# A new order for the operands of the pooled output product, in the lists of four engines

## The reference

```
def pool_mixer(x, w_in, w_grp, scale, w_out):
    h = x @ w_in
    u, z = h[..., :D_POOL], h[..., D_POOL:]
    ...                      # windowed means of u in four groups of 512 columns
    m = jnp.stack(outs, axis=2).astype(x.dtype)
    m = jnp.einsum('bsgc,gcd->bsgd', m, w_grp).reshape(B, S, D_POOL) * scale
    return (m * jax.nn.silu(z)) @ w_out
...
x = layer_norm(DN_ALPHA * x + y, ln_g[i], ln_b[i])
```

## Time and profile before

| | before |
|---|---|
| median of 3 runs | 1892.69 us (1892.03 to 1895.65) |
| the profiled execution | 1892.69 us, span from first to last instruction 1890.9 us |
| PE busy | 1832.0 us, 97% |
| DVE, POOL, ACT busy | 1368.0, 1079.6, 640.4 us |
| granted TensorE clock, mean | 0.995 |
| stage of the change (group product of group 0 to the last product of group 2) | 1621.8 to 1808.7 us of the span |

### The profile page before, as it was taken

The page is one execution under the profiler, slowest core; times in us unless marked ns, Lnnn a source line. Parts: engine busy times, 40 slices in busy tenths (PEclk is TensorE's granted clock), DMA queues, the critical chain, the costliest instruction groups (busy, mean ns, idle before and its releaser), DMA issues. The chain is left out here.

```text
span 1890.9 us, 23532 instructions
## 1 busy us (share of the span) xinstructions
PE 1832.0 (97%) x8904; PEld 1538.9 (81%) x8904; DVE 1368.0 (72%) x1530; ACT 640.4 (34%) x1128; POOL 1079.6 (57%) x780
## 2 busy tenths in 40 slices
PE   7999999999999999999999999999999999999996
PEld 6889889987887888888877888787788888788875
DVE  6777135566677776586589989567888876799886
ACT  4422157773331111111133433415433343323314
POOL 3443322253039988798876875532565465577655
PEclk9999999999999999999999999999999999999998
DMA  6111110013231143233377441113233231943122
GB/s 174 45 48 44 52 21 20 20 56 123 90 101 64 59 145 112 78 112 112 111 266 250 152 134 45 45 45 122 94 112 108 101 134 73 350 155 108 71 89 89
DMA packets 121698, 195.25 MB, mean 103 GB/s; under 512 B 30064, under 2 KB 85872, under 8 KB 118528
## 3 DMA queue, kind: packets, MB, share of 16 engines
q1 hardware_dynamic: 121424, 193.34, 30.1%
q10 hardware_dynamic: 176, 0.59, 0.1%
HBM read 145.08 MB, written 48.82 MB: 103 GB/s over the span
## 5 line engine op out<-in xcount | busy, mean ns | idle before, releaser
L1106 PE MATMUL ps<-f_hi,ring_hi 128*128 128x512 f32 x384 | 149.7, 390 | 1.3 <-POOL ring_lo L983 1.3
L1106 PE MATMUL ps<-f_lo,ring_hi 128*128 128x512 f32 x384 | 149.4, 389 | 0.0
L1106 PE MATMUL ps<-f_hi,ring_lo 128*128 128x512 f32 x384 | 149.4, 389 | 0.0
L893 POOL TENSOR_TENSOR w_lo<-stage,w_hi 128x1024 fp32r<-128x1024 f32 x48 | 124.7, 2598 | 4.0
L1106 PE MATMUL ps<-d_w_hi,d_hid_hi 128*128 128x512 f32 x312 | 121.8, 390 | 4.2 <-DVE y L2602 1.4
L1106 PE MATMUL ps<-d_w_hi,d_hid_lo 128*128 128x512 f32 x312 | 121.5, 389 | 0.0
L1106 PE MATMUL ps<-d_w_lo,d_hid_hi 128*128 128x512 f32 x312 | 121.4, 389 | 0.0
L983 POOL TENSOR_TENSOR ring_lo<-w_sum,ring_hi 128x512 fp32r<-128x512 f32 x80 | 117.2, 1465 | 6.7
L890 POOL TENSOR_TENSOR cols<-ones 128x1 f32<-128x1 f32 x48 | 26.1, 544 | 164.8 <-PE ps L1106 146.8
L1046 POOL TENSOR_TENSOR ring_lo<-w_sum,ring_hi 128x512 fp32r<-128x512 f32 x60 | 94.6, 1586 | 42.9 <-ACT ring_hi L2007 42.9
L1907 ACT ACTIVATE f_copy<-ps 128x512 f32<-128x512 f32 x60 | 35.3, 597 | 223.8 <-PE ps L1106 204.9
(11 more groups left out here) (442 smaller groups left out, 5707.1 us busy)
## 6 DMA issues: line engine op xcount, KB each, us to landing
d_raw<-hid_rows SPq DMA_DIRECT2D x37, 512.0 KB, 4.4
stage<-in_w_up SPq DMA_DIRECT2D x22, 512.0 KB, 4.5
wd_raw<-in_w_down SPq DMA_DIRECT2D x22, 512.0 KB, 4.9
raw_w<-in_w_gate SPq DMA_DIRECT2D x20, 512.0 KB, 4.9
stage<-in_w_in SPq DMA_DIRECT2D x18, 512.0 KB, 3.7
stage<-in_pool_w_in SPq DMA_DIRECT2D x16, 512.0 KB, 5.1
raw_w<-in_pool_w_in SPq DMA_DIRECT2D x16, 512.0 KB, 5.0
m_rows<-u_row SPq DMA_DIRECT2D x16, 512.0 KB, 2.6
```

The lines of the kernel that those rows point to most:

```text
L893: g.tensor_tensor(lo, stage[:, h, :], hi.bitcast(F32), ALU.subtract).then_inc(parted[h], 1)
L1106: last = mm(out_ap, l, r, start=(start and j == 0), stop=(stop and j == n - 1), skip_group_check=onto)
```

## The change

The same operations are done. What is changed is where some of them stand in four lists.

- **SP.** In the last round of the stage before (i = 7), the four loads of `wo_raw` for group 0 stood before the store of `z_buf`, in the block order 0, 2, 1, 3. They now stand behind it, in the order 0, 1, 3, 2.
- **DVE.** In group 0 the four `out_sums` stood after `gated` 4, after `gated` 6, after Q1's additions and after Q6's; in the groups 1 and 2 the first three stood after `gated` 1, 2, 3, and the fourth after Q6's additions. Now all groups have them after `gated` 1, 2, 3 and 4. The four `pool_rows_lo` of the next group stood after Q2 (one), Q7 (two) and Q3 (one); now they stand after Q5, Q7, Q3 and Q4, one each. The twelve `out_both_add` stood two after Q3, four after Q4 and six among the `gated` of group 3; now they stand two after Q7, three after Q3, three after Q4 and four in group 3.
- **ACT.** The high part of Q6's weights now comes before the rows of Q2, and the four `pool_rows_hi`, which stood in one piece after Q5's rows, are spread behind Q7 (two), Q3 and Q4.
- **POOL.** The low parts of Q2's and Q6's weights each move ahead of one operation on rows.

```
@@ sp_program, round i == 7
                     z_load(0, 0)
                     z_load(0, 1)
-                    sp.wait_ge(prod_full, quad_full(LAST_Q, 5))
-                    for b in (0, 2, 1, 3):
-                        wo_load(0, b)
                 sp.wait_ge(zs_ready, 4 * i + 4)
                 sp.dma_start(z_dram[i], z_buf[:].rearrange("p b n -> p (b n)")).then_inc(z_stored, 16)
...
+            sp.wait_ge(prod_full, quad_full(LAST_Q, 5))
+            for b in (0, 1, 3, 2):
+                wo_load(0, b)
@@ pool_program
                 out_weight_lo(i, Q1)
+                out_weight_lo(i, Q2)
                 out_rows_lo(i, Q1)
-                out_weight_lo(i, Q2)
+                out_weight_lo(i, Q6)
                 out_rows_lo(i, Q2)
-                out_weight_lo(i, Q6)
                 out_weight_lo(i, Q5)
@@ act_program
                 out_rows_hi(g, Q1)
+                out_weight_hi(g, Q6)
                 out_rows_hi(g, Q2)
-                out_weight_hi(g, Q6)
                 out_weight_hi(g, Q5)
                 out_rows_hi(g, Q6)
                 out_rows_hi(g, Q5)
-                pool_rows_hi(g + 1)
-                for o in (Q7, Q3, Q4):
-                    out_weight_hi(g, o)
-                    out_rows_hi(g, o)
+                out_weight_hi(g, Q7)
+                out_rows_hi(g, Q7)
+                pool_rows_hi(g + 1, (0, 1))
+                out_weight_hi(g, Q3)
+                out_rows_hi(g, Q3)
+                pool_rows_hi(g + 1, (2,))
+                out_weight_hi(g, Q4)
+                out_rows_hi(g, Q4)
+                pool_rows_hi(g + 1, (3,))
@@ dve_program
-            SUMS_AFTER = ((4, 6), (1, 2, 3))
-            BOTH = {Q3: (0, 1), Q4: (2, 3, 4, 5)}
...
                     gated(g, j)
-                    if j in SUMS_AFTER[g > 0]:
-                        out_sums(g, SUMS_AFTER[g > 0].index(j))
+                    if 1 <= j <= 3:
+                        out_sums(g, j - 1)
+                    if j == 4:
+                        out_sums(g, 3)
...
-                        if g == 0:
-                            out_sums(g, 2)
                     if o == Q2:
                         g_sums(g, 3)
-                        pool_rows_lo(g + 1, 0)
                     if o == Q6:
                         out_rows_low(g, Q7)
-                        out_sums(g, 3)
                     if o == Q5:
                         out_rows_low(g, Q3)
-                    if o == Q7:
-                        pool_rows_lo(g + 1, 1)
-                        pool_rows_lo(g + 1, 2)
-                    if o == Q3:
-                        pool_rows_lo(g + 1, 3)
-                    if g == STD_G - 1:
-                        for j in BOTH.get(o, ()):
+                    if o >= Q5:
+                        pool_rows_lo(g + 1, o - Q5)
+                    if g == STD_G - 1 and o >= Q7:
+                        for j in ((), (0, 1), (2, 3, 4), (5, 6, 7))[o - Q5]:
                             out_both_add(j)
```

More of the change, by code:

```diff
@@ L760, in z_load @@
                 sp.dma_start(z_in[:, e, :, :].rearrange("p b n -> p (b n)"), z_dram[2 * g + e]).then_inc(z_back, 16)
-            def wo_load(g, b):
-                r0, n = GW * PHASE[g] + 256 * (b // 2), b % 2
-                src = pw_out[r0:r0 + 256, n * HALF:(n + 1) * HALF].rearrange("(k p) n -> p k n", p=P)
-                sp.dma_start(wo_raw[b][:], src).then_inc(wd_in[b], 16)
             load(T_PG, cols_tile(w_pg, 0))
@@ L803, in sp_program, with wo_load @@
                     z_load(0, 1)
-                    sp.wait_ge(prod_full, quad_full(LAST_Q, 5))
-                    for b in (0, 2, 1, 3):
-                        wo_load(0, b)
                 sp.wait_ge(zs_ready, 4 * i + 4)
                 sp.dma_start(z_dram[i], z_buf[:].rearrange("p b n -> p (b n)")).then_inc(z_stored, 16)
+            def wo_load(g, b):
+                r0, n = GW * PHASE[g] + 256 * (b // 2), b % 2
+                src = pw_out[r0:r0 + 256, n * HALF:(n + 1) * HALF].rearrange("(k p) n -> p k n", p=P)
+                sp.dma_start(wo_raw[b][:], src).then_inc(wd_in[b], 16)
+            sp.wait_ge(prod_full, quad_full(LAST_Q, 5))
+            for b in (0, 1, 3, 2):
+                wo_load(0, b)
             sp.wait_ge(prod_full, quad_full(LAST_Q, 6))
@@ L2062, in first_block_rows, with pool_rows_hi @@
                 f(u_row[0][:, HALO:HALO + HALF], ps[:, 0, :], ACT.Copy).then_inc(c11_ready, 1)
-            def pool_rows_hi(g):
+            def pool_rows_hi(g, parts=range(4)):
                 if g:
                     act.wait_ge(grp_full, 8 * g)
-                for k in range(4):
+                for k in parts:
                     if k % 2 == 0:
@@ L2937, in dve_program @@
                     gated_low(j - 1)
-                if j < 6:
-                    out_both_add(6 + j)
+                if j < 4:
+                    out_both_add(8 + j)
             gated_low(7)
```

## The result

The changed kernel took 1913.01 us (median of four, 1910.16 to 1913.95), the kernel before 1893.56 beside it (four, 1892.03 to 1895.65). The ratio is 1.0099, 95% interval 1.0082 to 1.0117: slower by 1%. The forecast was 1910.4, range 1900 to 1918.

What follows compares the result with a forecast made beforehand. PE, busy 1832.0 of 1890.9 us, was taken as the bound, so only its gaps matter. The terms 4.1 + 13.4 − 2.5 − 0.5 + 3.2 = +17.7 us on 1892.69 gave 1910.4 us, range 1900 to 1918.

Steps and rivals of the forecast that it cites:

- a: First copy to `y_both` in group 0 starts later, lengthening PE's gap before Q2: +4.1 us.
- b: Starts of groups 1, 2, 3 wait for the fourth `m_lo`, now behind Q4's additions: +13.4 us, bounds 6.3 and 17.
- c: PE's waits at Q3 and Q4 go, as ACT's and POOL's weights come earlier: −2.5 us, bounds −2.5 and 0.
- d: The final stage's wait for `g_lo` goes, DVE having two `out_both_add` fewer there: −0.5 us, bounds −0.5 and 0.
- e: PE's clock falls behind two of three new group-start gaps, 1.6 us each: +3.2 us, bounds 0 and 4.8.
- the walk: Operation-by-operation timing in group 0, with DVE and POOL collisions, from block 2's landing to the first copy at 1655.0.
- The bare price of 2.1 us: At each next group's start, cost of `m_lo` behind PE's last block even with DVE ready: 2.1 us, three times.
- the first: Rival: DVE keeps up, fewer collisions, first copy about unmoved, only 2.1 us per group paid: +4.9, 1897.6 us; chance 0.12.
- The second: Rival: collisions and clock at their worst, more lateness carried into group 3: +24.3, 1917 us; chance 0.12.
- The third: Rival: early sums win and PE's old gaps go: 1885.5 us, or 1891.8 with 2.1 us per group; chance 0.03.

Runs made afterwards that it cites:

- Experiments 4: Changed kernel with SP's loads as before (ahead of the store, order 0, 2, 1, 3): 1911.95 us, ratio 1.0088.
- experiment 5: Changed kernel with group 0's four `out_sums` back in their old places: 1907.83 us, ratio 1.0072.
- experiment 2: Kernel before with only the four `pool_rows_lo` (`m_lo`) moved, one each after Q5, Q7, Q3 and Q4: 1906.35 us, ratio 1.0054.
- Experiment 3: Changed kernel with only the fourth `m_lo` moved back ahead of Q4's additions, right behind the third: 1899.69 us, ratio 1.0031.
- experiment 8: Changed kernel with the twelve `out_both_add` in their old places: 1913.08 us, ratio 1.0098.
- experiment 6: Kernel before with only ACT's and POOL's lists as changed: 1902.45 us, ratio 1.0040.
- experiment 7: Kernel before with ACT's and POOL's lists as changed and, in groups 1 and 2, the fourth sum after `gated` 4: 1893.73 us, ratio 0.9997.
- Experiments 1: Changed kernel with the four `pool_rows_lo` (`m_lo`) back in their old places: 1899.14 us, ratio 1.0022.
- experiment 9: Kernel before with group 0's first two sums after `gated` 3 and 4 instead of 4 and 6: 1894.86 us, ratio 1.0001.

## Why the prediction was right, step by step

The gaps and slow steps in the stage, from the two profiled executions, against the terms of the sum:

| term | forecast | measured |
|---|---|---|
| a, the first copy in group 0 | +4.1 | +5.0 (gap 7.8 against 2.8) |
| b, starts of groups 1, 2, 3 | 3.7 + 2.5 + 7.2 = 13.4 | 4.2 + 2.9 + 4.6 = 11.6 |
| c, waits at Q3 and Q4 | -2.5 | -2.5 |
| d, the wait for `g_lo` | -0.5 | -0.7 |
| e, the clock | +3.2 | +5.0 |
| sum | +17.7 | +18.4 |

(c: the two Q3 gaps of 0.86 and 0.53, and 1.1 us of waits below 0.3; e: what is left of the 18.4 after the other four.) With 2.8 us ahead of the stage the profiled execution was 21.2 us longer; the medians differ by 19.5. The sum is nearer than its terms, and that is luck: b was 1.8 too high, a and e together 2.7 too low. The direction and the size rest on a and b, which held in their mechanism; c and d came out for other reasons than the stated ones.

**a held, link by link.** ACT's wait for block 2 ended at 1635.2 instead of 1634.4, and that 0.8 us is nearly all by which the copy was later than forecast (1655.9 against 1655.0). DVE stood still for POOL's low weights of Q6, the sum and `g_diff` collided, the two `z_in` sums did not, all as in the walk. Experiments 4 and 5 show the cause on both sides: without the new load order the gap is 4.1, without the early sums 2.7. The walk did not say that it takes both; what I had as one chain has a second one right under it, POOL's rows of Q2, which holds Q2 at the old 2.7 us.

**b held in its mechanism; one of its terms was mis-sized.** The bare price of 2.1 us for an operation behind PE's last block was not measured by itself. It is bounded from above by experiment 2's 2.67 and 2.75, where DVE had little lateness, and the 2.9 at group 2's start less its 0.7 of lateness is 2.2. Experiment 3 shows that it comes from the fourth `m_lo` alone. Into group 1 the working gives 2.2 and half of 2.3, some 3.4, where 3.7 was written; 4.2 and 3.2 were measured with the same instructions (experiment 8). The start of group 3 was put at 7.2 and was 4.6: the step that failed is the collisions of `out_both_add` with POOL's `part`. I had priced the three after Q3 at 4.2, two of them beside POOL, with 1.1 for half a collision in `m_lo`. They took 2.73, which is 0.9 over their price alone, and `m_lo` 1.21, which is alone. POOL's part for the last stage began at 1822.0, and it was POOL that waited for `m_lo`. The collisions fell on the three `out_both_add` behind the last `m_lo` (4.90), where they cost PE nothing. In experiment 8 the gap without the moved `out_both_add` is 3.4, so they are worth 1.1 us of it.

**c came out by the number; its reason was wrong in group 0 and incomplete in the others.** I put the end of the Q3 and Q4 waits down to ACT's order (Q7's weights without the four `m_hi` ahead of them). In group 0 that order changes nothing by itself, since Q7's weights wait for the third sum (experiment 6). In the changed kernel POOL's low weights of Q3 end at 1678.2, which is 53.7 us into the stage and hardly earlier than before (54.3), while Q3 starts 58.4 us into it: the wait is gone because a makes PE late. In experiment 5, where PE comes earlier, 0.5 us of it is back. In the groups 1 and 2 POOL does end earlier with the new lists, as forecast, by 2.4 us in experiment 6. But POOL's and DVE's collisions then make DVE's low rows of Q3 the last to come, and the wait grows; it takes the early fourth sum as well (experiment 7). Experiment 2 takes the waits away with ACT and POOL untouched, by one collision less in POOL's row. I had looked at the order of the lists only, and not at what lengthened the operations in them, nor at whether PE would be there to wait.

**d came out by the number, and its reason was wrong.** I had put the end of the wait for `g_lo` down to two `out_both_add` fewer on DVE. Experiments 1 and 3 have them as changed and the wait is back (0.8 and 0.9); experiments 2, 6, 7 and 8 have them as before, and there is none. In 2 and 8, as in the changed kernel, PE comes late to the last stage, behind a gap at the start of group 3. What takes the wait away in 6 and 7, where there is no such gap, stays open.

**e: two of the three new gaps brought a fall, as charged, but each was longer.** 1.6 us had been read from a fall of 3.4 us. These lasted 6.8 and cost 2.8 and 2.6. The gaps were longer too (4.0 and 4.4 us idle against 2.6), and in experiment 2 the gap of 5.1 us had a fall of 6.8 and those of 2.5 and 2.6 had falls of 3.4. But the length of the gap does not settle it: at the same start of group 3, 4.4 us idle was followed by a fall of 6.8 us in the changed kernel and of 3.4 us in experiments 4 and 5. That e came out near rests in part on this one execution.

Of the rivals, the first (DVE keeps up, 1897.6) fell on DVE's lateness, seen in the four additions at each group's end that run without a wait, and on term a (+5.0 where it had 0). The second (1917, group 3 at its worst) fell on that same term of b. The third, faster, fell on the fourth `m_lo`: even with it back in place (experiment 3) the gap before Q2 keeps the kernel 0.3% slower than before.

## What to carry to other kernels

In lists that run in order, look for the operation that the bottleneck engine needs next, and never put it behind one that waits for that engine's own last result: a 1.2 us operation there cost 2.9 to 4.6 us of gap per group, and 13.5 us in all with the clock. When an operand is late, ask first what lengthened the operation that makes it, before moving it in its own list. When a wait is gone after a change, ask whether the operand comes earlier or the bottleneck engine later: the wait at Q3 in group 0 went only because PE was late. And price a new early operation with the arrival of its input: sums ahead of late weights held up all the gating behind them.

## What the runs showed of the hardware

The granted clock falls for 3.4, 6.8 or 10.2 us, and the same gap does not always bring it down. In the changed kernel the idle time of 2.74 us before group 2 had no fall behind it; in experiments 4 and 5 the same start, with the same 2.74 us, had one of 3.4 us, and in experiment 9 a gap of 2.09 us had one. Experiment 1 had 10.2 us of slow clock around a gap of 7.45 us, from 1654.6 on, while PE still waited until 1658.85.

Nor is it the same from one execution to the next where the instructions are the same. Ahead of the stage, behind the gap of 3.23 us in the earlier trace rows, the clock stayed at 1.00 in the execution before. In that of the changed kernel it is at 0.50 for 6.8 us, the only fall ahead of the stage that the other execution does not have, and so the likely place of the 2.8 us:

```profile
1188.40:1195.20 6.80, 5.60 (x18) 4.76 (x19) 6.73 (x8) 1.79 (x3) 4.72 (x2) 0.50 0.01 2
```

In the eleven executions profiled after the forecast the stage starts between 1621.6 and 1628.5 us, though nothing ahead of it differs but SP's list. This is about the size of the smaller effects studied, so a change of 1 to 4 us is read from the gaps of the stage, and not from a few times. Where a gap ends with a wait for an engine that is not slowed, it is better read from the place of its end in the stage than from its length.
